# Products of the identity in four waits of TensorE, in a convolution and retention backbone

## What is computed

```python
mod_x = (silu_c @ ada_w[i] + ada_b[i])[:, None, :]      # 6 * 1024 numbers per layer
hx = modulate(rmsnorm(x, norm1_g[i]), sx1, cx1)

def conv_module(h, pw1_w, pw1_b, dw_w, dw_b, ln_g, ln_b, pw2_w, pw2_b):
    z = h @ pw1_w + pw1_b
    a, g = jnp.split(z, 2, axis=-1)
    u = a * jax.nn.sigmoid(g)
    u = dwconv(u, dw_w, dw_b)                            # 31 taps along the tokens
    u = jax.nn.silu(layernorm(u, ln_g, ln_b))
    return u @ pw2_w + pw2_b
```

## Time and profile before

| | |
|---|---|
| time, median of 3 runs | 1715.95 us (1714.82 to 1718.08) |
| the profiled execution's own time | 1716.24 us |
| its span | 1714.4 us |
| TensorE, products | 1661.9 us busy, 97% of the span, 9862 records |
| TensorE, weight loads | 1435.2 us, 84% |
| vector engine | 915.6 us, 53% |
| ScalarE | 656.5 us, 38% |
| GpSimd | 166.0 us, 10% |
| data moved | 165.6 MB, 97 GB/s |

### The profile page before, as it was taken

How to read it: one execution, slowest core, us unless ns; L and a number is a source line. 1 busy time by engine, 2 the same in 40 slices (tenths; PEclk the granted TensorE clock), 3 DMA queues, 4 the chain that set the end, 5 groups by cost and what they waited for, 6 DMA issues and landing times.

```text
span 1714.4 us, 25097 instructions
## 1 busy us (share of the span) xinstructions
PE 1661.9 (97%) x9862; PEld 1435.2 (84%) x9862; DVE 915.6 (53%) x1473; ACT 656.5 (38%) x995; POOL 166.0 (10%) x171
## 2 busy tenths in 40 slices
PE   5899978999999999999999999999999999999998
PEld 3577747998888888888899898989898888888888
DVE  6699987574433433234358463544445744443444
ACT  4555647543322322223255231313133533332334
POOL 1288870000000000000000000000000000000000
PEclk8999989999999999999999999999999999999999
DMA  8777771122132122221213221211212324333321
GB/s 305 229 242 242 244 245 50 50 62 65 47 98 62 51 71 62 62 74 49 62 50 90 60 70 38 76 55 50 56 50 86 87 76 120 98 87 109 98 86 50
DMA packets 239822, 165.63 MB, mean 97 GB/s; under 512 B 5289, under 2 KB 215065, under 8 KB 239737
## 3 DMA queue, kind: packets, MB, share of 16 engines
q1 hardware_dynamic: 236168, 151.48, 29.4%
q0 software_dynamic: 2704, 9.83, 1.8%
q10 hardware_dynamic: 864, 3.15, 0.5%
HBM read 162.34 MB, written 2.10 MB: 96 GB/s over the span
## 4 chain that ended last, share of the span: by engine, by line
PE 82%; POOL 8%; DVE 4%; issue 2%; ACT 2%; DMA 0%; POOLq 0%; DVEq 0%; ACTq 0%
PE ps L605 81%; POOL odd_row L566 6%; DVE H_lo L1560 1%; POOL odd_row L576 0%; DVE w_lo L1519 0%; POOL conv L573 0%; POOL conv L580 0%; DVE rstd L1525 0%; DMA ada<-in_ada_w 0%; POOL even_row L566 0%; DVE conv L1793 0%; DVE tmp L1548 0%; DVE rstd L1536 0%; DVE sq L1548 0%; ACT tmp L1257 0%
## 5 line engine op out<-in xcount | busy, mean ns | idle before, releaser
L605 PE MATMUL ps<-H_hi,w_hi 128*128 128x512 f32 (+1 forms) x1712 | 586.6, 343 | 15.6 <-DVE H_lo L1622 8.1
L605 PE MATMUL ps<-H_lo,w_hi 128*128 128x512 f32 (+1 forms) x1712 | 580.7, 339 | 0.0
L605 PE MATMUL ps<-H_hi,w_lo 128*128 128x512 f32 (+1 forms) x1712 | 580.1, 339 | 0.0
L605 PEld LDWEIGHTS ps<-H_hi,w_hi 128*128 128x128 f32 x1712 | 326.6, 191 | 70.7 <-issue 27.4
L1519 DVE TENSOR_TENSOR w_lo<-w_raw,w_hi 128x1024 fp32r<-128x1024 f32 x208 | 255.3, 1241 | 194.4 <-ACT w_hi L1078 161.5
L605 PEld LDWEIGHTS ps<-H_hi,w_lo 128*128 128x128 f32 x1712 | 326.8, 191 | 35.2
L605 PEld LDWEIGHTS ps<-H_lo,w_hi 128*128 128x128 f32 x1712 | 327.1, 191 | 34.2
L605 PE MATMUL ps<-mid_hi,w_hi 128*128 128x512 f32 (+1 forms) x592 | 199.4, 337 | 0.6
L605 PE MATMUL ps<-mid_lo,w_hi 128*128 128x512 f32 (+1 forms) x592 | 198.3, 335 | 0.0
L605 PE MATMUL ps<-mid_hi,w_lo 128*128 128x512 f32 (+1 forms) x592 | 198.1, 335 | 0.0
L1962 DVE SCALAR_TENSOR_TENSOR tmp<-ps,par,tmp 128x511 f32<-128x511 f32 x66 | 41.6, 658 | 231.3 <-ACT tmp L1418 155.0
(11 more groups left out here) (225 smaller groups left out, 1921.8 us busy)
## 6 DMA issues: line engine op xcount, KB each, us to landing
w_raw<-in_ffn_w_in SPq DMA_DIRECT2D x88, 512.0 KB, 3.9
ada<-in_ada_w SPq DMA_DIRECT2D x40, 1024.0 KB, 6.0
w_raw<-in_ret_w_in SPq DMA_DIRECT2D x40, 512.0 KB, 3.9
w_raw<-in_ffn_w_out SPq DMA_DIRECT2D x32, 512.0 KB, 4.4
w_raw<-in_conv_pw_w SPq DMA_DIRECT2D x24, 512.0 KB, 8.8
w_raw<-in_ffn_w_out SPq DMA_DIRECT2D x16, 384.0 KB, 3.6
ada<-in_ada_w POOLq DMA_DIRECT2D x4, 1024.0 KB, 8.9
w_raw<-in_ret_w_out SPq DMA_DIRECT2D x8, 512.0 KB, 4.3
```

The costliest lines, as they stand in the source:

```text
L605: return nc.tensor.matmul(o, a, b, start=first, stop=last, skip_group_check=True)
```

## The change

A helper keep_warm(bank, n) issues n products of the 128 by 128 identity with itself, into the first 128 columns of a PSUM bank. It waits for nothing and signals nothing, and what it writes is read by nobody: the next real use of each bank starts a new sum. It is called four times in TensorE's program: 10 products into bank 7 after the last token transposes, 12 into bank 6 after the second modulation transposes, 12 into bank 1 ahead of the last tile's means in the layer norm, and 10 into bank 6 after the sums of squares. Nothing else differs, and no other engine's program changes.

```diff
@@ -816,6 +816,11 @@
+            def keep_warm(bank, n):
+
+                for _ in range(n):
+                    mm(ps[:, bank, 0:P], ident[:], ident[:], True, True)
+
@@ -828,6 +833,7 @@
             par_transposes([(0, 128), (1, 116)], 6)
             token_transposes(2)
+            keep_warm(7, 10)
             pe.wait_ge(filled, 4)
             pe.wait_ge(diag_ready, 1)
             mm(ps[:, 4, :], mean_of[:], flat_sq[:, LATS], True, True)
@@ -840,6 +846,7 @@
             ada_transposes(0)
             ada_products(1)
             ada_transposes(1)
+            keep_warm(6, 12)
 
             def first_block(h, k0, k1):
 
@@ -895,6 +902,7 @@
                 if j == KT - 1:
                     ada_transposes(20)
                     ada_products(21)
+                    keep_warm(1, 12)
 
                 pe.wait_ge(conv_ready, j + 1)
                 mm(slot(0, 0), mean_of[:], conv[:, j, 0:LAT], j == 0, j == KT - 1)
@@ -909,6 +917,7 @@
                 variance(t)
 
             src = (H_hi, H_lo)
+            keep_warm(6, 10)
             for t in range(3):
                 for i in range(4):
                     n = 4 * t + i
```

## The result

The changed kernel takes 1719.84 us, the median of 22 executions (1715.11 to 1721.46), and the kernel before on the same chip 1716.93 (22 executions, 1714.82 to 1718.97). The medians lie 2.9 us apart and the means 2.4, with a standard error of 0.4. The ratio, which goes with the means, is 1.0014 with an interval of 1.0008 to 1.0020: 0.14% slower, where 1714.4 and no difference were forecast, and outside the range of 1711.3 to 1718.6. The effect is under the 0.2% that I called no change, but its interval leaves out zero.

What follows compares the result with a forecast made beforehand. TensorE, nearly full, was the bound after an opening and layer norm of waits at lowered clock. Opening +0.3, layer norm -2.1 and last fill 0 made -1.8 us from 1716.24: 1714.4 us, range 1711.3 to 1718.6, no difference expected.

Steps and rivals of the forecast that it cites:

- the landing of the weight: Opening: first projection weight, slowed by group 3's earlier load, lands between 32 and 37.3 us, taken as 35; w_lo 1.3 later.
- the term of the opening: Everything before the first H_hi products: +1.3 us collision less 1.0 from full clock, +0.3 us; bounds -2.4 and +2.6.
- the gap at 29 us: DMA queues: up to 0.9 us with q0 dry lets up to 450 of some 600 remaining weight packets through.
- fill 1: Ten products at 18.8 us: 2.1 to 2.5 us inside the wait; sums at 22.68 fall from 2.9 us to 1.5.
- Rival (c): Opening: weight lands at 36 or later, TensorE waits until 41, first products at 1.2 GHz, +2.6; 1718.0 us, chance 0.13.
- the rule weighed there: Trainium skill: transposes don't count as TensorE activity, so the first fill would start at 1.2 GHz and give nothing; prediction disagreed.
- Fill 2: Twelve products before the first H_hi product at about 40.1 us: 2.6 to 2.9 us at full clock, about 1.0 back.
- Fill 3: Twelve products at 247.1 us in the layer norm: faster mean and squares sums, -2.1 us; bounds -2.3 and +0.4.
- Rival (b): Layer norm: clock falls in the 2 us left idle, gain -0.8 instead of -2.1; 1715.7 us, chance 0.25 with the collision.
- Fill 4: Ten products before 272.2 us: 2.1 to 2.5 us in 3.83 of idle; range -0.2 to +0.8, taken as 0.
- Rival (a): Opening: the load's packets find the weight already through, no collision; -2.4 and -2.1 make -4.5, 1711.7 us, chance 0.17.
- The frame: Starting time of the sum: the profiled execution's 1716.24 us, 0.3 above the median of the runs shown, 1715.95.

Runs made afterwards that it cites:

- e1: The changed kernel with all four fills, unchanged, run again for a second profile: 1719.54 us, ratio 1.0010 to the kernel before.
- e14: The kernel before plus the opening's two fills only, group 3's load left early: 1721.39 us, ratio 1.0023.
- e13: The changed kernel without its last fill (10 products after the sums of squares), group 3's load left early: 1720.20 us, ratio 1.0009.
- e15: The changed kernel with 30 products instead of 12 in the fill after the second modulation transposes: 1718.12 us, ratio 1.0005 to the kernel before.
- e3: The kernel before plus the first fill alone (10 products after the last token transposes): 1721.30 us, ratio 1.0025.
- e6: The changed kernel with only its first and third fills, group 3's load held until the first weights landed: 1715.58 us, ratio 0.9992 to the kernel before.
- e7: The changed kernel without its last fill, group 3's load held until the first weights landed: 1714.57 us, ratio 0.9981 to the kernel before.
- e2: The changed kernel, all four fills, plus GpSimd holding group 3's load until the first weights landed: 1714.52 us, ratio 0.9984 to the kernel before.
- e8: The changed kernel with only the opening's two fills, group 3's load held until the first weights landed: 1715.34 us, ratio 0.9986 to the kernel before.
- e9: The kernel before plus the third fill alone (12 products ahead of the last tile's means): 1717.43 us, ratio 0.9998.
- e5: The kernel before plus only the wait holding group 3's load until the first weights landed, no fill: 1718.22 us, ratio 1.0005.
- e4: The kernel before plus the layer norm's two fills only, opening as before: 1716.73 us, ratio 0.9991.
- e10: The kernel before plus the last fill alone (10 products after the sums of squares): 1719.95 us, ratio 1.0013.
- e16: First three fills, group 3's load held, plus identity products behind paced steps of the first blocks of both projections: 1713.85 us, ratio 0.9980 to the kernel before.

## Why the prediction was wrong

**The step that failed is the landing of the weight.** The prediction had "the weight lands between 32 and 37.3; I take 35", and w_lo 1.3 us later than before. ScalarE took the weight at 36.76 in e1 and at 35.95 to 37.20 in the others, so w_lo started at 37.91 in e1, 2.9 us later than the 34.99 of the earlier trace rows and outside the bound of +2.6 that I gave it. In the sum it is the term of the opening, +0.3 us, that was mis-sized: the two fills of the opening alone (e14) measure +3.6 (error 0.6). The bound itself was worked out wrongly. If a landing at 35 makes w_lo 1.3 us late, my own latest landing of 37.3 makes it 3.6 us late, not 2.6; with that, the upper end of the range would have stood a microsecond higher, at 1719.6, still just under what was measured. I had allowed up to 450 packets of the weight to slip into the gap at 29 us. The six profiles with fill 1 and the load early, from the issue of the load and q1's packets in the microsecond from 29 to ScalarE's take-up: 25.54, 471 and 34.22 (the fastest run); 25.43, 360 and 37.08 (e14); 25.36, 362 and 35.95 (e13); 25.07, 210 and 36.76 (e1); 25.04, 170 and 37.15 (e15); 24.93, 132 and 37.20 (e3). So a later issue leaves more of a gap, but as many as 360 packets through it still left the weight over 36 once: the packets' sum doesn't set the landing alone. In e14 876 packets of q1 passed from 29 to 36, where some 600 of this weight were left, and it landed at 37.05; so some of them were already the second weight's. That the slowest of the 16 engines sets the landing, as I had put it, fits this but isn't shown engine by engine. My forecast was the good end of a distribution, and I had taken it for its middle.

**Rival (c) is what mostly happened, and its condition was put right:** a landing at about 36, TensorE waiting until 41, the clock gone, the first products at 1.2 GHz. I gave it 0.13, because I let the gap take up to 450 of the 600 packets left. The late landing came in 5 profiles of 6 and the wait until 40.9 to 42.2 with it; the first H_hi product at the lower clock came in e1, e3 and e14 (0.76 and 0.77 us), while in e13, and behind the long fill of e15, it took 0.47 and the clock fell right after it. Its price of +2.6 in the opening was too small. The ada_half products moved by +3.3 in e1 and +3.7 in e3, and where the clock fell once more in the stretch behind 60 us, the loss there was 5.5 us (68.39 against 62.90). The windows at 58 to 62 and 62 to 66 of before, and at 62 to 66 of e1:

```profile
58.00:62.00 4.00, 3.26 (x15) 2.26 (x16) 2.87 (x6) 1.81 (x3) 0.00 (x0) 1.00 0.67 164
62.00:66.00 4.00, 4.00 (x30) 2.23 (x29) 1.28 (x9) 1.09 (x2) 0.00 (x0) 1.00 0.21 29
```
```profile
62.00:66.00 4.00, 4.00 (x9) 2.70 (x10) 2.88 (x5) 1.59 (x3) 0.00 (x0) 0.50 0.63 154
```

**Fill 1 itself was right**: inside its wait, at full clock (2.40 us forecast as 2.1 to 2.5), sums of 2.9 us turned into 1.5. The cost was in what a faster TensorE releases, as the prediction had it. On the rule weighed there, that full clock doesn't engage in a stretch of transposes (the Trainium skill, page "TensorE: Matmul & The Clock Gate", section "Part 4: PE-mode transpose"): the twenty records right behind the transposes ran at 0.12 us each in every profile with fill 1, so the trace again disagrees. The halved spacing of the transposes, which the prediction cites for it, is not itself a change of the granted clock: that reads 1.00 from 6 to 18 us in before, in the slower rows too. What paced those isn't shown.

**Fill 2** was forecast at -1.0 us, if the first H_hi product stays near 40.1. The condition failed, since that product came at 41 to 42 in the usual case. It is shown the other way round by e6 and e7: with the weight early, fill 2 gives 1.6 us (error 0.7), and in their profiles the way from the first H_hi product to ada_half takes 4.16 and 3.16, the very 1.0 us of the sum. The fill itself ran at full clock in 3 profiles of 10 only (e1, e2, e15: 0.11 to 0.12 us a record); in the others its 24 records took 3.7 to 4.5 us, still inside the wait.

**Fill 3** was forecast at -2.1, and -2.2 is what the profile of before gives against most others: from the last mean sums to the first H_hi product it takes 20.37 us in before (251.83 to 272.20) and 18.17 in nine of the eleven profiles with fill 3. But before is near the long end: the seven profiles without the fill run from 19.30 to 20.67, 20.07 on average, those with it average 18.39, and so 1.7 us is the fairer figure. Rival (b), a clock that falls in the 2 us left, was seen in e13, where the last mean sums took 2.82 us, and in part in e6 (1.93). Over many executions fill 3 gave 0.8 to 1.5 us (e7 less e8, e13 less e14), each with an error of about 0.7; alone, in e9, 0.26. In the profiles e9 is 2.8 us ahead of e5 at group 22 and 1.2 at the end; most of what goes is the place at 1341 us, 75.36 us in e9 and 74.15 in e5.

**Fill 4** at nothing holds for the changed kernel (e13). In the fastest run of the change the stretch behind it gave back 1.1 us (280.12 is only 1.0 ahead of 281.12, where 270.12 was 2.1 ahead), as it did in e7 and e13 without the fill.

**Rival (a), no collision,** is what e2 built: forecast -4.5 us for it against its own frame, measured -3.0 as a mean. Between the profiled spans it is -4.9, but e2's profile is of its fastest execution, 1711.78 us, where the next took 1714.11.

**The frame.** The prediction was made from an execution of 1716.24 us that stood 0.3 above the median of three. Over 22 executions the median before is 1716.93, and 1716.1 to 1718.2 in the other batches. Of the 5.4 us between 1714.4 and 1719.84, 0.7 is this frame. The opening is 3.3 (+3.6 in e14 for +0.3), and a layer norm that gave 0.8 to 1.5 us for 2.1 makes about 1; the rest is within the errors.

## What to carry to other kernels

Ahead of making one engine faster in a prologue, list what its progress releases, and on which queue: a load issued 2.2 to 2.8 us early cost 4.8 us here, by taking turns with small packets on which everything waited. In this kernel, filling the opening's idle stretches paid only where the transfer behind them was safe; the fix is one wait (or an earlier issue), worth nothing alone and 5 us with the fills. And where a transfer slips through a gap of one microsecond, a single profile, above all that of the fastest run, tells one end of a distribution; take another before you explain.

## What was not expected

**One opening takes two courses, 2 to 2.7 us apart.** In one batch the 33 times of the kernel before run from 1714.88 to 1719.62, with clusters at 1715.2 and 1719.0 and more between. The profiles of e4, e9 and e10 have the program of before up to 62 us, e5 nearly so, and they reach its 62.90 row at 64.9 to 65.6. The windows of e5 (load held, no fill) at that place:

```profile
54.00:58.00 4.00, 1.69 (x11) 1.26 (x9) 3.90 (x12) 3.34 (x6) 0.00 (x0) 1.00 1.06 392
58.00:62.00 4.00, 3.37 (x9) 2.01 (x8) 3.35 (x5) 2.19 (x4) 0.00 (x0) 0.52 0.91 224
62.00:66.00 4.00, 4.00 (x20) 3.28 (x22) 1.63 (x9) 0.44 (x1) 0.00 (x0) 0.63 0.02 4
```

Before, at a clock of 1.00 in 58 to 62, has 3.26 us busy there; e5, at 0.52, 3.37, and 0.63 in the window behind; e9 and e10 have 0.50 in 58 to 62. Before and e5 had both waited 2.3 us for H_lo just ahead (2.29 before 56.50, 2.31 before 57.33). The same idle stretch is followed by either clock, so the moment of the fall isn't a function of the program alone. I have no run that shows what sets it. Even e7 and e2, with all their idle stretches filled in the opening, are 4 to 5 us apart between their fastest and slowest executions (1711.37 to 1716.14, 1711.78 to 1715.65).

**A full clock at the start of a paced stretch can come out as a loss.** Before, the low clock lay under waits that cost nothing. In e10 and in the fastest run of the change the low stretch lay 2 to 3 us further on behind the first H_hi product, over products that bind. From that product to group 22 the six profiles that start at the lower clock take 8.79 to 9.07 us. Of the eleven that start at full clock, e16 again left aside, six take 8.48 to 8.71 and five 9.57 to 10.28. Keeping a clock only up to the point where work gets sparse won a third of a microsecond or lost one, in about equal numbers.

**One place at 1341 us is worth up to 2.7 us, and no experiment touched it.** Every profile has the same 2.20 to 2.22 us of idle there, and the 401 records behind it take from 72.64 us (e3) to 75.36 (e9, e15), 73.9 to 74.2 in most. It is the second place where like idle is followed by unlike clocks, and the program is the same there in all kernels.
